# A two-layer hybrid encoder on one core: every third low part of a weight granule on GpSimd

## The reference, cut to what matters

```python
for l in range(DEPTH):                      # DEPTH = 2, SEQ = 256, D_MODEL = 2048
    h = _rmsnorm(x, norm_g[l])
    z = h @ w_in[l]                         # one wide input projection
    (rq, rk, rv, rg, gq, gk, gv, gg, ga_f, ga_b, pv, pg, mq, mkv, mkr, mg) = jnp.split(z, points, axis=-1)
    y_a = _retention_branch(rq, rk, rv, rg, ...)     # chunked retention, head norm, SiLU gate
    y_b = _gla_branch(gq, gk, gv, gg, ga_f, ga_b, ...)
    y_c = _pool_branch(pv, pg, ...)
    y_d = _mla_branch(mq, mkv, mkr, mg, ...)         # latent attention, wq_b and wkv_b projections
    x = x + jnp.concatenate([y_a, y_b, y_c, y_d], -1) @ w_out[l]
```

## Time and profile before

| | before |
|---|---|
| median of three runs | 845.27 us |
| span of the profiled execution | 843.8 us |
| TensorE matmul busy | 829.3 us (98%) |
| VectorE busy | 464.5 us (55%) |
| ScalarE busy | 428.4 us (51%) |
| GpSimd busy | 50.2 us (6%) |
| mean granted TensorE clock | 0.996 |

### The profile page before, as it was taken

How to read it: one execution, slowest core, us unless ns; L and a number is a source line. 1 busy time by engine, 2 the same in 40 slices (tenths; PEclk the granted TensorE clock), 3 DMA queues, 4 the chain that set the end, 5 groups by cost and what they waited for, 6 DMA issues and landing times.

```text
span 843.8 us, 11480 instructions
## 1 busy us (share of the span) xinstructions
PE 829.3 (98%) x4084; PEld 701.4 (83%) x4084; DVE 464.5 (55%) x611; ACT 428.4 (51%) x616; POOL 50.2 (6%) x44
## 2 busy tenths in 40 slices
PE   6999999999999999999989999999999999999998
PEld 5898888888888888888869888888878888888886
DVE  2554497445375853654445635864653649546542
ACT  4864565456725543433347655663475345444441
POOL 6110000000000101000122000000000010010000
PEclk9999999999999999999989999999999999999999
DMA  8765764533543454565436656644354345546654
GB/s 343 251 230 190 240 215 150 174 125 126 175 150 125 147 178 150 193 206 198 156 117 227 246 186 227 198 150 150 125 175 147 128 147 162 176 139 204 194 186 140
DMA packets 41924, 150.67 MB, mean 179 GB/s; under 512 B 4752, under 2 KB 4880, under 8 KB 41744
## 3 DMA queue, kind: packets, MB, share of 16 engines
q1 hardware_dynamic: 40592, 145.25, 51.5%
q0 software_dynamic: 432, 2.88, 0.8%
q10 hardware_dynamic: 848, 1.83, 0.7%
HBM read 147.85 MB, written 2.10 MB: 178 GB/s over the span
## 4 chain that ended last, share of the span: by engine, by line
PE 96%; ACT 1%; issue 1%; DMA 1%; DVE 1%; SPq 0%; ACTq 0%; DVEq 0%
PE pair L357 84%; PE bank L388 4%; PE bank L637 1%; PE bank L611 1%; PE bank L500 1%; PE bank L679 1%; PE bank L669 1%; PE bank L592 1%; DMA raw<-stream 1%; PE bank L627 0%; PE bank L548 0%; PE bank L570 0%; PE bank L560 0%; ACT gate L731 0%; DVE lo L978 0%
## 5 line engine op out<-in xcount | busy, mean ns | idle before, releaser
L978 DVE TENSOR_TENSOR lo<-raw,hi 128x1024 fp32r<-128x1024 f32 (+3 forms) x266 | 307.3, 1178 | 213.1 <-ACT hi L713 209.2
L713 ACT ACTIVATE hi<-raw 128x1024 fp32r<-128x1024 f32 (+3 forms) x272 | 270.4, 1022 | 155.7 <-PE pair L357 132.5
L357 PE MATMUL pair<-lo,xT_hi 128*128 128x512 f32 (+1 forms) x768 | 296.9, 387 | 2.4 <-DVE xT_lo L995 2.4
L357 PE MATMUL pair<-hi,xT_hi 128*128 128x512 f32 (+1 forms) x768 | 296.0, 396 | 2.9 <-ACT xT_hi L747 2.6
L357 PE MATMUL pair<-hi,xT_lo 128*128 128x512 f32 (+1 forms) x768 | 296.9, 387 | 0.0
L357 PEld LDWEIGHTS pair<-lo,xT_hi 128*128 128x128 f32 x768 | 145.5, 189 | 30.2 <-issue 3.3
L357 PEld LDWEIGHTS pair<-hi,xT_hi 128*128 128x128 f32 x768 | 144.3, 189 | 30.4 <-ACT xT_hi L747 3.3
L357 PEld LDWEIGHTS pair<-hi,xT_lo 128*128 128x128 f32 x768 | 145.2, 189 | 28.5
L357 PE MATMUL pair<-hi,yT_hi 128*128 128x512 f32 (+1 forms) x304 | 116.7, 384 | 0.0
L357 PE MATMUL pair<-hi,yT_lo 128*128 128x512 f32 (+1 forms) x304 | 116.6, 383 | 0.0
L357 PE MATMUL pair<-lo,yT_hi 128*128 128x512 f32 (+1 forms) x304 | 116.5, 383 | 0.0
(11 more groups left out here) (138 smaller groups left out, 519.7 us busy)
## 6 DMA issues: line engine op xcount, KB each, us to landing
raw<-stream SPq DMA_DIRECT2D x272, 512.0 KB, 4.2
out<-x SPq DMA_DIRECT2D x8, 256.0 KB, 5.3
consts<-consts_in POOLq DMA_DIRECT2D x1, 1792.0 KB, 14.9
mats<-mats_in ACTq DMA_DIRECT2D x2, 576.0 KB, 3.5
x<-x_in POOLq DMA_DIRECT2D x2, 512.0 KB, 9.3
x<-x_in SPq DMA_DIRECT2D x1, 512.0 KB, 4.6
x<-x_in ACTq DMA_DIRECT2D x1, 512.0 KB, 9.0
consts<-consts_in ACTq DMA_DIRECT2D x1, 64.0 KB, 4.3
```

Source lines behind the costliest of these rows:

```text
L357: return nc.tensor.matmul(pair[a][m][:, 0:width], x_part[:, slots[i], m * P:(m + 1) * P], w_part[r][:, i * 512:i * 512 + width], start=(sl ...
L713: nc.scalar.activation(cut[0], cut[1], ACT.Copy).then_inc(rounded[r].sem, 1)
L978: nc.vector.tensor_tensor(cut[0], cut[1], cut[2].bitcast(F32), ALU.subtract).then_inc(split[r].sem, 1)
```

## The change

GpSimd takes the low part of granules 0, 1, 2 and of every j with j % 3 == 2 to the end of the layer, 47 of 136 per layer where it had 3; VectorE skips these. GpSimd's roots keep their order and stand between its `splits` calls.

```diff
+def on_pool(j):
+    return j < POOL_SPLITS or j % 3 == 2
...
@@ VectorE
                 def splits(upto):
                     for j in range(pos[0], upto):
+                        if on_pool(j):
+                            continue
                         r = j % RING
                         dve.wait_ge(*rounded[r].at(l, j // RING + 1))
@@ GpSimd
-                for j in range(POOL_SPLITS):
-                    pool.wait_ge(*rounded[j].at(l, 1))
-                    pool.tensor_tensor(lo[j][:], raw[j][:], hi[j][:].bitcast(F32), ALU.subtract
-                                       ).then_inc(split[j].sem, 1)
+                pos = [0]
+                def splits(upto):
+                    for j in range(pos[0], upto):
+                        if not on_pool(j):
+                            continue
+                        r = j % RING
+                        pool.wait_ge(*rounded[r].at(l, j // RING + 1))
+                        per, width = len(PLAN[j][1]), STAGES[PLAN[j][0]][0]
+                        cut = [t[r][:].rearrange("p (i n) -> p i n", i=2)[:, 0:per, 0:width] for t in (lo, raw, hi)]
+                        pool.tensor_tensor(cut[0], cut[1], cut[2].bitcast(F32), ALU.subtract
+                                           ).then_inc(split[r].sem, 1)
+                    pos[0] = upto
+                splits(10)
                 pool.wait_ge(consts_loaded.sem, 16)
                 rsqrt(x_ms, x_rs, x_ms_ready, x_rs_ready)
+                splits(12)
                 pool.wait_ge(*mats_loaded.at(l, 16))
...
+                splits(13)
                 rsqrt(lq_ms, lq_rs, lq_ms_ready, lq_rs_ready)
+                splits(20)
                 rsqrt(lk_ms, lk_rs, lk_ms_ready, lk_rs_ready)
+                splits(37)
                 rsqrt(q_ms, q_rs, q_ms_ready, q_rs_ready)
+                splits(44)
                 rsqrt(k_ms, k_rs, k_ms_ready, k_rs_ready)
+                splits(87)
                 rsqrt(o_ms, o_rs, ob_ms_ready, ob_rs_ready)
+                splits(104)
                 rsqrt(o_ms, o_rs, oa_ms_ready, oa_rs_ready)
+                splits(GRANULES)
```

More of the change, by code:

```diff
@@ L1354, in _ @@
                 pool.wait_ge(cleared.sem, 5)
-                for j in range(POOL_SPLITS):
-                    pool.wait_ge(*rounded[j].at(l, 1))
-                    pool.tensor_tensor(lo[j][:], raw[j][:], hi[j][:].bitcast(F32), ALU.subtract
-                                       ).then_inc(split[j].sem, 1)
+                pos = [0]
[9 more added lines that the diff above has]
+                                           ).then_inc(split[r].sem, 1)
+                    assert pos[0] <= upto
+                    pos[0] = upto
+                splits(10)
                 pool.wait_ge(consts_loaded.sem, 16)
                 rsqrt(x_ms, x_rs, x_ms_ready, x_rs_ready)
+                splits(12)
                 pool.wait_ge(*mats_loaded.at(l, 16))
```

## The result

| | before | after |
|---|---|---|
| median of the runs | 845.25 us (4 runs) | 852.55 us (4 runs) |
| ratio, 95% interval | | 1.0086 (1.0072 to 1.0100) |
| span of the profiled execution | 843.8 us | 850.7 us (the execution took 852.51) |
| mean granted TensorE clock there | 0.996 | 0.995 |

The account below looks back on a forecast made before the run. TensorE's own work, 98% busy, was taken as the bound. Late granules of 3.2 us per layer, 6.4 in two, made the span 850.2 from 843.8, and 851.6 us with 1.5 outside; own range 848.5 to 853.5, wider 846.5 to 855.5.

Parts of the forecast that it names:

- What bounds the kernel: TensorE's own work, busy 98% of the span; VectorE's freed time was counted as 0 gain, at best 0.6 us.
- The 1.5 us: Time outside the profiled span, added to the forecast span of 850.2 to make 851.6 us.
- Granules 11, 26, 68: GpSimd's longer subtractions there end after the matmul is due: 0.25, 0.42 and 0.12 us late per layer.
- Granule 104: GpSimd's low part, behind branch A's root and then held by VectorE's granule 105: 0.78 us late per layer.
- Granule 44: GpSimd's low part behind the root of k: 0.60 us late if VectorE goes first, 0 if GpSimd; 0.30 taken.
- Granule 94: VectorE's low part, delayed by GpSimd's granules 92 and 95: 1.3 us late per layer, bounds 0 and 1.9.
- Rivals 1 and 2: GpSimd waits for VectorE, never the reverse: 849.6 us, chance 0.22; or meetings cost nothing worth telling: 847.7 us, chance 0.12.
- rival 3: The clock falls at a 1.3 us stall too: each layer loses 3.2 us more, 858 us; chance 0.06.
- rival 4: The lags at granules 11, 26, 68 go and meetings fall out well: within 1.7 us, 846 us; chance 0.13.
- rival 5: At the turn of the layer VectorE's shorter program restarts sooner and the clock holds: 842.8 us; chance 0.07.

Follow-up runs that it names:

- e1: The changed kernel with granules 11, 26, 68, 92, 95 and 104 back on VectorE: 845.12 us, ratio 1.0001 to the kernel before.
- e9: The changed kernel without granules 11, 26, 68 and 95 on GpSimd, granule 104 ahead of branch A's root, VectorE's layer loop written out twice: 840.91 us.
- e4: The kernel before with granules 11, 26 and 68 alone moved to GpSimd: 846.77 us, ratio 1.0023.
- e3: The changed kernel with GpSimd's granule 104 ahead of the root for branch A: 849.98 us, ratio 1.0066 to the kernel before.
- e6: The changed kernel with granule 92 alone back on VectorE: 849.36 us, ratio 1.0062 to the kernel before.
- e7: The changed kernel with GpSimd writing zeros by memset for granules 92 and 95, their subtraction left out: 849.41 us, ratio 1.0063 to the kernel before.
- e5: The kernel before with granules 92 and 95 alone moved to GpSimd: 846.74 us, ratio 1.0034.
- e8: The kernel before with VectorE's loop over the layers written out twice, other engines keeping theirs: 840.97 us, ratio 0.9960.

## Why the prediction was right

- **What bounds the kernel.** Right. TensorE's own work sets the time, and VectorE's 62 us less changed nothing (e1, e9). The 1.5 us that were added for launch and end come from two different executions; in each single one of before and after it is 1.8 us (852.51 less 850.7). That changes no difference.
- **Granules 11, 26, 68.** Right in place and mechanism (e4). Granule 26 was forecast 0.1 us too small: the time from GpSimd's end (81.04) to the first matmul (81.19) is 0.15 us there, and not the 0.05 of the earlier trace rows. At granules 11 and 68 it is 0.05 and 0.06.
- **Granule 104.** Right to the hundredth: the root of 1.64 us, then GpSimd held by VectorE's granule 105 (2.78 us in place of 2.38) (e3 takes it away).
- **Granule 44.** Wrong by 0.30 us per layer, the middle that I took between two orders. GpSimd was first in both layers (its subtraction at 120.65, VectorE's line 1094 at 120.72, then 3.40 us long), and that order costs nothing. GpSimd goes straight on to its next instruction, while VectorE waits for the root's semaphore. In both layers GpSimd came first by 0.07 us, and that decided.
- **Granule 94.** Right: 1.3 us forecast, 1.36 and 1.33 measured. The assumption behind it, that the lock holds in both directions, was the one that no row of before showed. It was an assumption that came true. Line 1274 beside the subtraction (3.43 us), and without it (1.22 us, e6 and e7), shows it. The Trainium skill's rule for it (page "SBUF — State Buffer", section "Who interferes with whom") is that a Vector instruction with two SBUF inputs and a GpSimd instruction that reads SBUF exclude each other, and that the order of issue decides which one is blocked. The rows agree in both directions (3.43 us for 1.22 on VectorE, 2.78 for 2.38 on GpSimd). The rule leaves out GpSimd instructions that only write. e7's memset (0.95 us beside VectorE and alone) agrees with that in the one order that it had. Rivals 1 and 2, by which VectorE is not held, fall.
- **The term that was missing** is the slower start after a stall, 0.6 us per layer. The sum was 6.4 us for both layers, and the traces have 7.3. The lateness itself came to 6.1 in place of 6.4 (granule 44 brought 0.6 less, granules 26, 94 and 68 together some 0.3 more), and 1.2 for the slower starts were not in the sum. That the total came within 1 us is in part luck: two errors of opposite sign.
- **The clock** (rival 3) did not fall at stalls of 1.36 us: the one digit 8 is the turn's, as before. Its price per fall, 3.2 us, is 2.9 by the traces of before and e5. **Hidden after all** (rival 4) holds for 41 granules, but for 0.1 to 0.2 us a layer, and not for the six. **The turn** (rival 5) was not changed by the shorter program: VectorE idle for 3.33 and 3.36 us. (The prediction read the 3.33 in brackets as the time since the input was there; it is the engine's idle time, from the end of its last addition at 423.17. The input came 2.6 us ahead of the start. That changes no term of the sum.) That the restart is the loop's is shown by e8, but the change doesn't act on it.
- GpSimd's busy time was forecast as some 250 us and is 261.8; VectorE's fell by 61.5 us and not by 100, since time held up counts as busy.

## What to carry to other kernels

Where one engine is 98% busy and the others feed it through a ring, list for each moved piece when its input is there and when it is due, and compare with the new duration; shares of busy time say nothing. 38 of the 44 moved granules could take twice as long at next to no cost, and the moves of the six others made all but 0.1 to 0.2 us per layer of the loss. Which granules j % 3 == 2 picks is chance: by the prediction's own sum, as an estimate from the trace of before, granules 18, 39, 69, 82, 84 and 91 would have come 0.4 to 1.2 us late, and the change happened to leave them on VectorE. And a subtraction on GpSimd is not a free-standing piece of work: it and an instruction of VectorE with both inputs in SBUF stop each other, so what matters is which of the two is issued first at each meeting, down to 0.1 us, and a hidden delay at one meeting can turn round the order at the next.

## What the runs showed of the hardware that was not expected

- At a hardware loop's end VectorE stood idle for 3.3 us between its last instruction and its first of the next pass, the last 2.6 of them with its input ready. Written out twice, it starts 0.1 us after its input, and the kernel is 3.6 us faster (e8), though the change under study had nothing to do with it.
- The clock does not always fall at the turn. The profiled execution of e5 has TensorE standing 2.3 us for VectorE there like all others with the loop, and a clock of 1.000 throughout; so had 2 of 12 runs of the kernel before. What decides it is open.
- The first matmul after a stall is 0.1 us longer, and the one behind it starts as much later, even after a stall of 0.15 us (granule 68), and behind granule 49 with no stall that the starts show.
